# A fused two-block layer: the latent queries' squares in four buffers, their sums ahead of the norms, the recurrent gates behind all query blocks, and the gate rows turned inside the gate panel

## The reference, cut to what matters

```python
proj = h @ w_in
u, v_m, o_pre, i_pre, f_pre, c_q, c_kv, k_r = split(proj)
ig, fg = i_pre + b_igate, f_pre + b_fgate          # recurrent gates
logf = log_sigmoid(fg); b = cumsum(logf)           # along the tokens
y_m = sigmoid(o_pre) * norm(mlstm(q_m, k_m, v_m, ig, fg))

q_a = (rmsnorm(c_q) @ w_uq).reshape(S, A_HEADS, 192)
kv  = (rmsnorm(c_kv) @ w_ukv).reshape(S, A_HEADS, 256)
q_nope = rmsnorm(q_a[..., :128]); q_rope = rope(rmsnorm(q_a[..., 128:]))
k_nope = rmsnorm(kv[..., :128]);  v_a = kv[..., 128:]
y_a = norm(causal_attention(q, k, v_a))
x = x + concat(y_m, y_a) @ w_out
```

## Time and profile before

| | us |
|---|---|
| median of three runs | 1905.22 |
| lowest and highest | 1904.64, 1906.01 |
| the profiled execution | 1907.58 |
| its span, first to last instruction | 1905.9 |
| PE busy | 1856.4 (97%) |
| POOL, DVE, ACT busy | 1361.9, 878.1, 742.6 |

### The profile page before, as it was taken

One profiled execution on the slowest core, in us unless ns is written; L12 is line 12 of the kernel. 1 busy time (PEld: TensorE's weight loads), 2 busy tenths in 40 slices (PEclk: granted clock), 3 DMA queues, 4 the chain that ended last, 5 costly groups with the idle time before them and its releaser, 6 DMA issues.

```text
span 1905.9 us, 26543 instructions
## 1 busy us (share of the span) xinstructions
PE 1856.4 (97%) x9787; PEld 1577.3 (83%) x9787; DVE 878.1 (46%) x1733; ACT 742.6 (39%) x1393; POOL 1361.9 (71%) x1207
## 2 busy tenths in 40 slices
PE   7999999999999999989999999898999999999999
PEld 6888888888878888878888888798678878888887
DVE  6677777762024544455502421637663455203410
ACT  4577777754025572232101210367643522101200
POOL 8766666798844457978888988754245669988985
PEclk9999999999999999989999999899999999999999
DMA  7322222223332222422332333222013222333332
GB/s 218 110 67 67 67 67 67 67 67 110 112 98 62 66 64 89 134 67 89 98 101 89 102 96 89 66 73 78 23 61 117 85 71 89 88 101 98 88 105 72
DMA packets 213614, 165.73 MB, mean 87 GB/s; under 512 B 14478, under 2 KB 209873, under 8 KB 213122
## 3 DMA queue, kind: packets, MB, share of 16 engines
q1 hardware_dynamic: 208134, 149.32, 26.9%
q10 hardware_dynamic: 5372, 14.98, 2.4%
HBM read 161.11 MB, written 7.37 MB: 88 GB/s over the span
## 4 chain that ended last, share of the span: by engine, by line
PE 86%; POOL 4%; PEld 3%; ACT 3%; DVE 2%; issue 1%; PEldq 0%; ACTq 0%; POOLq 0%; DVEq 0%
PE bank L401 58%; PE bank L473 9%; PE bank L420 3%; POOL w_lo L3020 3%; PEld bank L401 2%; PE bank L1562 2%; PE bank L1538 2%; PE bank L443 1%; PE bank L1548 1%; PE bank L1204 1%; PE bank L1150 1%; PE bank L1201 1%; POOL w_hi L3012 1%; ACT w_hi L1385 1%; PE bank L1180 1%
## 5 line engine op out<-in xcount | busy, mean ns | idle before, releaser
L3020 POOL TENSOR_TENSOR w_lo<-w_raw,w_hi 128x512 fp32r<-128x512 f32 (+1 forms) x576 | 721.7, 1284 | 215.0 <-ACT w_hi L1385 205.6
L3012 POOL TENSOR_TENSOR w_hi<-w_raw,one 128x512 fp32r<-128x512 f32 (+1 forms) x428 | 439.6, 1058 | 248.1 <-PE bank L401 212.1
L401 PE MATMUL bank<-h_hi,w_hi 128*128 128x512 f32 x952 | 382.0, 401 | 0.7 <-POOL w_lo L3020 0.4
L401 PE MATMUL bank<-h_hi,w_lo 128*128 128x512 f32 x952 | 372.1, 391 | 0.0
L401 PE MATMUL bank<-h_lo,w_hi 128*128 128x512 f32 x952 | 371.1, 390 | 0.0
L401 PE MATMUL bank<-a_hi,w_hi 128*128 128x512 f32 x832 | 326.0, 392 | 1.8 <-POOL w_lo L3020 1.4
L401 PE MATMUL bank<-a_hi,w_lo 128*128 128x512 f32 x832 | 324.0, 389 | 0.0
L401 PE MATMUL bank<-a_lo,w_hi 128*128 128x512 f32 x832 | 323.8, 389 | 0.0
L401 PEld LDWEIGHTS bank<-h_hi,w_lo 128*128 128x128 f32 x952 | 178.6, 188 | 38.9
L401 PEld LDWEIGHTS bank<-h_hi,w_hi 128*128 128x128 f32 x952 | 179.1, 188 | 35.0 <-POOL w_lo L3020 1.0
L401 PEld LDWEIGHTS bank<-h_lo,w_hi 128*128 128x128 f32 x952 | 179.2, 188 | 33.8
(11 more groups left out here) (471 smaller groups left out, 2986.8 us busy)
## 6 DMA issues: line engine op xcount, KB each, us to landing
w_raw<-in_w_ff SPq DMA_DIRECT2D x32, 1024.0 KB, 5.6
w_raw<-in_w_in SPq DMA_DIRECT2D x31, 1024.0 KB, 5.4
w_raw<-in_w_mlp_in SPq DMA_DIRECT2D x16, 1024.0 KB, 5.4
w_raw<-in_w_mlp_out SPq DMA_DIRECT2D x16, 1024.0 KB, 5.7
w_raw<-in_w_in SPq DMA_DIRECT2D x26, 512.0 KB, 4.2
w_raw<-in_w_ssd_out SPq DMA_DIRECT2D x8, 1024.0 KB, 5.7
bias_rows<-bias_row ACTq DMA_DIRECT2D x1, 4096.0 KB, 15.6
w_raw<-in_w_attn_out SPq DMA_DIRECT2D x4, 1024.0 KB, 4.9
```

Source lines behind the costliest of these rows:

```text
L401: mm = pe.matmul(bank[:, 0:ntok], a, b[:, koff + k, 0:ntok], start=(k == 0 and n == 0), stop=(k == L.kb - 1 and n == 2))
L3012: pool.tensor_tensor(w_hi[:, slot, part], raw[:, slot, part], one[:].broadcast_to([P, n]), ALU.mult).then_inc(split_hi, 1)
L3020: ins = pool.tensor_tensor(w_lo[:, slot, part], raw[:, slot, part], w_hi[:, slot, part].bitcast(F32), ALU.subtract)
```

## The change

Three things are changed, none of them in the arithmetic.

1. `SQUARES` gets two more buffers, in the first two rows of `decay_moving`, a tile that is last read in the first block of the layer (a second, unrounded name for the same memory is declared ahead of it). ACT's square of block i waits for the sums of block i-4 and no longer of block i-2.
2. The gates move on ACT behind the last root, on DVE behind the last sums. On DVE all sums stand ahead of the norms, except for the norm of token block 0, which stands behind the sums of block 5.
3. On PE the eight row transposes move from ahead of the gate panel to between its two blocks, and ACT reads the panel's first block ahead of the rows.

```diff
-        SQUARES = [a_free_hi[:, 3, :], a_free_hi[:, 12, :]]
+        SQUARES = [a_free_hi[:, 3, :], a_free_hi[:, 12, :], moving_plain[:, 0, :], moving_plain[:, 1, :]]
...
-            if i >= 2:
-                act.wait_ge(lt["red"], i - 1)
-            act.activation(SQUARES[i % 2][:, 0:384], bank, ACT.Square).then_inc(acc_free, 1)
+            if i >= 4:
+                act.wait_ge(lt["red"], i - 3)
+            act.activation(SQUARES[i % 4][:, 0:384], bank, ACT.Square).then_inc(acc_free, 1)
...
-            sq = SQUARES[i % 2][:, 0:384].rearrange("p (h f) -> p h f", h=2)
+            sq = SQUARES[i % 4][:, 0:384].rearrange("p (h f) -> p h f", h=2)
...
+            pe_panel_tokens(pe, L_gate_m[0], 0, 0, h_x, only=0)
             pe.wait_ge(ml["dve"], 3)
             for bank, part in ((banks[5], GATE_PARTS[6]), (banks[6], GATES[:, :, 0:M_HEADS])):
                 for t in range(T):
                     mm = pe.transpose(bank[0:M_HEADS, t * P:(t + 1) * P], part[:, t, :], ident[:])
             mm.then_inc(ml["rows"], 1)
-            pe_panel_tokens(pe, L_gate_m[0], 0, 0, h_x)
+            pe_panel_tokens(pe, L_gate_m[0], 0, 0, h_x, only=1)
...
                 q_block_act(act, i)
-                if i == 1:
-                    gates_act(act)
                 if i >= 3 and i % 2:
                     q_root_act(act, (i - 3) // 2)
             q_root_act(act, T - 1)
+            gates_act(act)
+            tokens_act(act, L_gate_m[0], 0, lambda t: OM[:, t, 0:256], ACT.Sigmoid, only=0)
             act.wait_ge(ml["rows"], 1)
...
-            tokens_act(act, L_gate_m[0], 0, lambda t: OM[:, t, 0:256], ACT.Sigmoid)
+            tokens_act(act, L_gate_m[0], 0, lambda t: OM[:, t, 0:256], ACT.Sigmoid, only=1)
...
                 q_sums_dve(dve, i)
-                if i == 1:
-                    gates_dve(dve)
-                if i >= 3 and i % 2:
-                    q_norm_dve(dve, (i - 3) // 2)
-            q_norm_dve(dve, T - 1)
+                if i == 5:
+                    q_norm_dve(dve, 0)
+            gates_dve(dve)
+            for t in range(1, T):
+                q_norm_dve(dve, t)
```

More of the change, by code:

```diff
@@ L101, in build_program @@
         small = sb("small", [P, 128])
+        with nc.sbuf_tensor("decay_moving_plain", [P, 2 * T - 1, S], F32) as moving_plain:
+            pass
         moving = sb("decay_moving", [P, 2 * T - 1, S], F32R)
```

## The result

The changed kernel took 1910.99 us in the median of nine runs (1908.41 to 1912.41), the kernel before 1905.22 us beside it. The ratio is 1.0026, with a 95% interval from 1.0018 to 1.0035: slower by about 5 us (5.8 us between the medians), little but clear of no change. The profiled execution took 1912.41 us, 1910.7 of them its span.

A forecast was written before the change was run, and what follows sets the result against it. PE, busy for 97% of the span, was taken to bound the kernel. To the median of 1905.22 us it added +2.7 (slowed norm) and +2.5 (clock falls), +5.2, giving 1910.4 us; range 1905.7 to 1911.8 us.

The forecast's parts named there:

- The wait that goes: PE ahead of query block 6: the 1.29 us wait goes, and PE stands at the row transposes at 1300.9.
- The prediction's other side: Rival: gates through before PE needs them, end before 1302.6; at best -3 us, 1902.2 us; chance 0.04.
- The gates' end: Gates on DVE and ACT, behind a norm slowed by POOL: end at 1305.8, or 1303.8 if not slowed.
- The hole: PE at the row transposes waits for the gates from 1300.9 to 1305.8, 4.9 us in place of 1.29.
- What comes back: ACT reads one half early, 0.72 us less; first key block still 2.7 us late, carried to the end.
- The clock: TensorE's clock falls at PE's hole: 2.2 us on the second gate half plus 0.3 on transposes, 2.5 us.
- The two holes it was read from: PE's two 5.3 us waits before L420, where the granted clock fell to 0.50; taken as agreeing with the idle-stretch rule.
- the sentence that an idle stretch brings the clock down: TensorE's clock: by the skill's rule an idle stretch brings it down; the trace was said to agree at both holes.
- the clock staying up: Rival at PE's hole: norm slowed but the clock does not fall; +2.7, 1907.9 us; chance 0.33.
- The case of a norm that is not slowed: Rival on DVE: norm not slowed, PE's hole 2.9 us, clock stays up; +0.7, 1905.9 us; chance 0.15.

The follow-up runs named there:

- two sets: The changed kernel against the kernel before, timed twice: 1910.99 us in nine runs (ratio 1.0026), 1910.24 us in eleven (1.0025).
- the filled hole: Changed kernel with 36 more matmuls of 256 columns on PE ahead of its wait at the row transposes, into an unread bank: 1908.04 us.
- holes of 3.15 and 2.83 us: Changed kernel with row transposes behind the whole gate panel, 1908.70 us; changed kernel with POOL's key panel split held until the gates are done, 1907.85 us.
- the hole of 10.4 us: Changed kernel with the row transposes ahead of both halves of the gate panel again: 1916.66 us in four runs.
- Its sister's: Changed kernel with rows behind both halves, POOL's second gate panel split held until the norms are done, and token block 0's norm behind the gates: 1904.87 us.

## Why the prediction was right

The forecast was 1910.4 us by way of +2.7 us of waiting and +2.5 us of the clock. Measured were +5.8 and +4.9 us in two sets.

- **The wait that goes.** The 1.29 us ahead of query block 6 are gone, and PE reached the transposes at 1301.1, against 1300.9 in the sum. That two buffers would have done the same was shown. The prediction's other side, with the norm out of the way, was put at "at best -3 us"; undoing the norm's place does that, and gave 1.0 us in its trace and nothing that could be measured in its time.
- **The gates' end.** Counted 1305.8, found 1305.76 (1305.59 and 0.17; this trace's starts are 0.07 us above those of the earlier trace rows). Each step is within 0.2 us of where it was put: L2266 at 1295.62 (1295.5), the sums of block 6 at 1299.25 (1299.3), ACT's table load at 1300.91 (1300.95, though the 0.5 us for the root, added to 1300.3, give 1300.8). This came from taking the slowed rows of the first norm and not the clean ones, since POOL's start moves with the last query block. With POOL held back it was 1.85 us less, against the 2.0 of the sum. In the Trainium skill, "SBUF — State Buffer", in the rules on the shared port pair, the DVE instruction with two SBUF inputs is the one that contends and a reduction never does. The trace agrees: L2257 took 0.41 us beside POOL as without.
- **The hole.** Counted 4.9 us, found 4.68.
- **What comes back.** The first key block was counted 2.7 us late without the clock; the filled hole gave 2.4 us. It went on to the end undiminished (621.6 us from the first query matmul to the end against 619.1), as I carried it.
- **The clock.** It fell, as in the forecast. Its price was 2.5 us in the sum; it was 2.0 us at the first key block and 2.3 us at the end (623.9 against 621.6). The size came about in another way. I took 4.9 us of dense work at half clock, and it was 2.8 us (1307.34 to behind 1310.1), which costs 1.3 us and not 2.2. The transposes cost 0.7 us and not 0.3. And the last 0.3 us are those of the second, short fall, which was in no case of the prediction. That 2.5 stands so near to 2.3 is in part luck.
- **The two holes it was read from.** At both L420 waits the clock had fallen before the long wait began, at the first by 829.30, where the wait began at 831.49 (836.83 less 5.34). PE had by then waited 1.44 us and done matmuls of one column. So these rows showed a fall after little work, not one in an idle hole, and did not bear out the sentence that an idle stretch brings the clock down. The changed kernel's trace does: the clock fell within the 4.68 us in which PE did nothing.

The chances had the fall at 0.43 and the clock staying up at 0.33. All profiled executions of the changed kernel and of its variants with a hole of 4.7 us or more (four in all) show the fall, and those with holes of 3.15 and 2.83 us did too. So it was surer than I said. The case of a norm that is not slowed (0.15) was too generous: L2266 started 0.08 us behind POOL's first instruction, and the norm's other steps lay under POOL as well, as the rows had it.

## What to carry to other kernels

Where a chain that runs to and fro between two engines ends in something that TensorE waits for, nothing that is not needed for it should stand ahead of it on either engine, and an instruction with two inputs in SBUF should not be put where POOL works, if something waits for what stands behind it. Price a moved instruction by what runs beside it at its new place; ask again which POOL work will have moved there, for a gain of 2 us upstream was lost to just that and came back with one wait on POOL. A hole on TensorE costs more than the time that PE is late by: here PE was 2.4 us late through waiting, and the low clock behind the hole of 4.68 us took 2.0 us more.

## What the hardware showed that I had not expected

A hole of 2.83 us was enough for the granted clock to fall in one profiled execution; the kernel before has no such fall at its waits of 1.3 us. In the hole of 10.4 us (1293.95 to 1304.35) it was at 1.00 for the first 4.8 us, where in the hole of 4.68 us it fell half way, so the length of a hole does not tell when the fall comes:

```profile
1294.00:1298.80 4.80, 0.00 (x0) 0.00 (x0) 4.70 (x10) 1.22 (x4) 4.71 (x7) 1.00 0.52 181
1299.00:1304.30 5.30, 0.00 (x0) 0.00 (x0) 2.46 (x15) 3.41 (x6) 0.80 (x2) 0.50 0.61 194
```

And the changed kernel's trace has a short fall in a stretch where PE's busy time looks high:

```profile
1455.00:1460.00 5.00, 4.74 (x42) 4.65 (x41) 1.33 (x1) 0.68 (x3) 4.95 (x4) 1.00 0.01 3
1460.50:1463.70 3.20, 3.20 (x17) 3.20 (x16) 0.00 (x0) 2.31 (x3) 0.72 (x1) 0.50 0.79 247
```

The busy time misleads here. From 1457.89 to 1460.00 PE started nothing but matmuls of one column (L631, L632), and then waited 0.26 us:

```profile
1459.38 0.36 PE L632 MATMUL bank<-one,arena 128*128 128x1 f32 x2
1460.00 0.38 PE L2787 MATMUL bank<-w_hi,h_hi 128*128 128x256 f32 x1 [0.26 <-POOL w_lo L3023]
```

The same fall stands in the second profile of the changed kernel and in that with two buffers, and costs 0.3 us in each: set against the kernel before, PE is 4.3 to 4.4 us late just ahead of it and 4.6 to 4.7 us late once it is over. The kernel before does the same one-column matmuls without a fall. The kernel with the rows behind the panel and POOL held has two like it, at 1452.5 and, behind a wait of 1.78 us, at 1544.7. In its profile they took the whole lead: PE leads the kernel before by 2.0 us ahead of the first, by 1.8 us between them and by 0.1 us after the second. Its sister's profile has neither and keeps 2.4 us. So they are a likely part of why the runs of both spread over 3.5 to 4 us. What brings them about was not tried.

In the kernel with the rows behind the panel, DVE's instructions with two inputs in SBUF took 1.26 to 1.54 us beside POOL's split, whatever their size (128x128 to 128x512), where alone they take 0.29 to 0.69. POOL's own four took 1.3 to 1.75 us (5.71 together, 4.99 in the run where they were held back): each DVE instruction took about as long as one of POOL's.
